# At six seams of a two-block kernel: scaled tiles in four buffers, scales issued ahead of the splits, transposes placed between the row-by-row products

## The reference, cut to what matters

```python
def first_block(x, c, ...):
    for l in range(2):
        sh_m, sc_m, gt_m, sh_f, sc_f, gt_f = split(silu(c) @ ada_w[l] + ada_b[l], 6)
        h = rmsnorm(x, norm_mix[l]) * (1 + sc_m) + sh_m          # seam ("mix", l)
        x = x + gt_m * hybrid_mixer(h, w_in[l], w_out[l], ...)   # attention, HGRN2, gated delta
        h = rmsnorm(x, norm_ffn[l]) * (1 + sc_f) + sh_f          # seam ("ffn", l)
        x = x + gt_f * ((silu(h @ w_gate[l]) * (h @ w_up[l])) @ w_down[l])

def second_block(x, mem, ...):
    for l in range(2):
        proj = x @ w_in_2[l]                                     # seam ("proj", l)
        out = merge(ssd(proj), diff_attention(proj), memory_attention(proj, mem)) @ w_out_2[l]
        x = layernorm(ALPHA * x + out, ln_g_2[l], ln_b_2[l])
```

## Time and profile before

| | |
|---|---|
| median of three runs | 4295.01 us |
| the three runs | 4287.96, 4295.93, 4295.01 us |
| span of the profiled execution (first to last instruction) | 4287.7 us |
| PE busy | 3992.2 us, 93% |
| DVE busy | 2571.8 us, 60% |
| ACT busy | 1621.0 us, 38% |
| mean granted clock of TensorE, share of full speed | 0.955 |

### The profile page before, as it was taken

One profiled execution on the slowest core, in us unless ns is written; L12 is line 12 of the kernel. 1 busy time (PEld: TensorE's weight loads), 2 busy tenths in 40 slices (PEclk: granted clock), 3 DMA queues, 4 the chain that ended last, 5 costly groups with the idle time before them and its releaser, 6 DMA issues.

```text
span 4287.7 us, 51835 instructions
## 1 busy us (share of the span) xinstructions
PE 3992.2 (93%) x20700; PEld 3250.2 (76%) x20700; DVE 2571.8 (60%) x4066; ACT 1621.0 (38%) x2881; POOL 108.0 (3%) x199
## 2 busy tenths in 40 slices
PE   5879999998889999999999999999899999999988
PEld 5759778877768788887777677767777777777776
DVE  6767365654576432456667743776566667546765
ACT  3343232243443332333444243553334343334532
POOL 0000000000000000000000000000000000000000
PEclk9979799998899799989999999999899999999999
DMA  6502155532111232333232223233232322221233
GB/s 219 171 5 89 50 168 196 188 118 65 60 40 69 72 101 84 106 100 104 91 99 72 74 89 94 64 104 126 80 119 85 108 70 84 84 88 56 84 113 113
DMA packets 216641, 417.93 MB, mean 97 GB/s; under 512 B 16384, under 2 KB 61472, under 8 KB 214608
## 3 DMA queue, kind: packets, MB, share of 16 engines
q1 hardware_dynamic: 197584, 335.12, 24.4%
q0 software_dynamic: 18816, 79.49, 5.4%
HBM read 378.89 MB, written 35.67 MB: 97 GB/s over the span
## 4 chain that ended last, share of the span: by engine, by line
PE 80%; DVE 12%; ACT 5%; issue 2%; DMA 1%; SPq 0%; DVEq 0%; ACTq 0%; POOLq 0%
PE ps L632 59%; PE ps L104 13%; DVE arena L126 3%; PE ps L115 3%; ACT arena L200 3%; DVE arena L141 2%; DVE spl L126 2%; PE ps L2292 2%; DVE X L126 1%; DVE HF L126 1%; DVE sm L147 1%; PE ps L2287 1%; ACT sph L200 1%; PE ps L882 1%; PE ps L110 1%
## 5 line engine op out<-in xcount | busy, mean ns | idle before, releaser
L126 DVE TENSOR_TENSOR spl<-ring,sph 128x1024 fp32r<-128x1024 f32 (+2 forms) x556 | 651.5, 1178 | 731.9 <-ACT sph L200 730.7
L200 ACT ACTIVATE sph<-ring 128x1024 fp32r<-128x1024 f32 (+2 forms) x556 | 562.4, 1023 | 776.6 <-PE ps L632 758.3
L632 PE MATMUL ps<-sph,HTh 128*128 128x512 f32 (+3 forms) x1680 | 668.9, 398 | 22.6 <-DVE HTl L126 11.7
L632 PE MATMUL ps<-spl,HTh 128*128 128x512 f32 (+3 forms) x1680 | 621.5, 370 | 0.0
L632 PE MATMUL ps<-sph,HTl 128*128 128x512 f32 (+3 forms) x1680 | 620.6, 369 | 0.0
L200 ACT ACTIVATE arena<-ps 128x512 f32<-128x512 f32 (+2 forms) x570 | 314.0, 563 | 727.8 <-PE ps L632 484.3
L632 PE MATMUL ps<-HTh,sph 128*128 128x512 f32 x1360 | 540.5, 397 | 17.1 <-DVE spl L126 14.9
L632 PE MATMUL ps<-HTl,sph 128*128 128x512 f32 x1360 | 532.5, 392 | 0.0
L632 PE MATMUL ps<-HTh,spl 128*128 128x512 f32 x1360 | 532.1, 391 | 0.0
L104 PE MATMUL ps<-arena 128*128 128x128 f32 (+6 forms) x2264 | 374.0, 349 | 52.3 <-ACT arena L200 29.9
L632 PE MATMUL ps<-sph 128*128 128x512 f32 x992 | 405.6, 409 | 7.4 <-DVE spl L126 7.4
(11 more groups left out here) (219 smaller groups left out, 5105.3 us busy)
## 6 DMA issues: line engine op xcount, KB each, us to landing
ring<-in_w_in SPq DMA_DIRECT2D x264, 512.0 KB, 3.6
arena<-in_ada_w SPq DMA_DIRECT2D x88, 512.0 KB, 4.7
ring<-in_w_down SPq DMA_DIRECT2D x44, 512.0 KB, 3.3
ring<-in_w_gate SPq DMA_DIRECT2D x40, 512.0 KB, 3.8
ring<-in_w_up SPq DMA_DIRECT2D x40, 512.0 KB, 3.8
ring<-in_w_mem SPq DMA_DIRECT2D x32, 512.0 KB, 3.3
ring<-in_w_out SPq DMA_DIRECT2D x32, 512.0 KB, 3.9
ring<-in_w_br_ssd SPq DMA_DIRECT2D x32, 512.0 KB, 3.9
```

The lines of the kernel that those rows point to most:

```text
L126: self.e.tensor_tensor(o, a, b, op).then_inc(*self.done.up())
L200: self.e.activation(o, a, f, **kw).then_inc(*self.done.up())
L632: ins = pe.e.matmul(o, l, r, start=k0 == 0 and i == 0 and not b.pairs, stop=k0 + b.ks == b.kt and i == 3 * b.ks - 1 and (c0 > 0 or not b.p ...
```

## The change

The scale's scratch grows from two buffers to four, in all three places where it is declared or used. On ACT the scale of tile k is issued ahead of the high half of tile k - 1, and on DVE the scale of tile k ahead of the rest of tile k - 2. The scales no longer wait for the engine's own last instruction. The rest of the second weight chunk moves from ahead of tile 2's scale to behind tile 2's rest, and that of the third from ahead of tile 4's scale to ahead of the rest of tile 7. On PE one turning stands ahead of each row k of the first products.

```diff
@@ first_products
             for k in range(b.ks):
+                next(turned[key], None)
                 pe.wait_ge(at[key, "hth", k], at[key, "htl", k])
...
             ins.then_inc(*pe.done.up())
-            for _ in range(b.ks):
-                next(turned[key], None)

         def ht_act(a, key, scale, bias, scr, marks=None):
-            for k in range(8):
-                if k == 4:
+            for k in range(9):
+                if k == 5:
                     warm_up(a, key, 2, 3)
-                f = scr[:, k % 2, :]
-                if scale is None:
-                    a.wait_ge(at[key, "htt", k])
-                    f = bank_of[key, "ht", k][:, :]
-                elif k % 2:
+                if scale is not None and k % 2:
                     bank = bank_of[key, "ht", k]
-                    a.wait_ge(at[key, "htt", k], at[key, "htl", k - 2] if k > 1 else None)
+                    a.wait_ge(at[key, "htt", k], at[key, "htl", k - 4] if k > 3 else None)
                     a.wait_ge(*[at[x] for x in marks(k)])
-                    t = a.act(f, bank[:, :], ACT.Identity, scale=scale[:, k:k + 1], bias=bias[:, k:k + 1], par=k > 1)
-                    at["free", (key, "ht", k)] = t
-                    a.wait_ge(t)
-                else:
-                    a.wait_ge(at[key, "htf", k])
-                at[key, "hth", k] = a.cp(HT[0][:, k, :], f, par=True)
+                    at[key, "htf", k] = at["free", (key, "ht", k)] = a.act(
+                        scr[:, k % 4, :], bank[:, :], ACT.Identity, scale=scale[:, k:k + 1], bias=bias[:, k:k + 1], par=True)
+                if k > 0:
+                    f = scr[:, (k - 1) % 4, :]
+                    if scale is None:
+                        a.wait_ge(at[key, "htt", k - 1])
+                        f = bank_of[key, "ht", k - 1][:, :]
+                    else:
+                        a.wait_ge(at[key, "htf", k - 1])
+                    at[key, "hth", k - 1] = a.cp(HT[0][:, k - 1, :], f, par=True)

         def ht_dve(v, key, scale, bias, scr):
-            for k in range(8):
-                if k in (0, 2, 4):
-                    warm_up(v, key, k // 2, k // 2 + 1)
-                f = scr[:, k % 2, :]
-                if scale is None:
-                    f = bank_of[key, "ht", k][:, :]
-                elif k % 2 == 0:
+            for k in range(10):
+                if k in (0, 5, 9):
+                    warm_up(v, key, k // 4, k // 4 + 1)
+                if scale is not None and k < 8 and k % 2 == 0:
                     bank = bank_of[key, "ht", k]
-                    v.wait_ge(at[key, "htt", k], at[key, "htl", k - 2] if k > 1 else None)
-                    t = v.ts(f, bank[:, :], scale[:, k:k + 1], bias[:, k:k + 1], ALU.mult, ALU.add, par=k > 1)
-                    at[key, "htf", k] = at["free", (key, "ht", k)] = t
-                v.wait_ge(at[key, "hth", k])
-                at[key, "htl", k] = v.tt(HT[1][:, k, :], f, HT[0][:, k, :].bitcast(F32), ALU.subtract, par=True)
+                    v.wait_ge(at[key, "htt", k], at[key, "htl", k - 4] if k > 3 else None)
+                    at[key, "htf", k] = at["free", (key, "ht", k)] = v.ts(
+                        scr[:, k % 4, :], bank[:, :], scale[:, k:k + 1], bias[:, k:k + 1], ALU.mult, ALU.add, par=True)
+                if k > 1:
+                    f = bank_of[key, "ht", k - 2][:, :] if scale is None else scr[:, (k - 2) % 4, :]
+                    v.wait_ge(at[key, "hth", k - 2], at[key, "htf", k - 2] if scale is not None else None)
+                    at[key, "htl", k - 2] = v.tt(HT[1][:, k - 2, :], f, HT[0][:, k - 2, :].bitcast(F32), ALU.subtract, par=True)
...
-            scr = ar(4096, 2, 512)
+            scr = ar(4096, 4, 512)
...
-            scr = ar(0, 2, 512)
+            scr = ar(0, 4, 512)
```

More of the change, by code:

```diff
@@ L905, in ht_act @@
-                at[key, "hth", k] = a.cp(HT[0][:, k, :], f, par=True)
-        def ht_dve(v, key, scale, bias, scr):
-            for k in range(8):
-                if k in (0, 2, 4):
-                    warm_up(v, key, k // 2, k // 2 + 1)
-                f = scr[:, k % 2, :]
-                if scale is None:
-                    f = bank_of[key, "ht", k][:, :]
-                elif k % 2 == 0:
-                    bank = bank_of[key, "ht", k]
-                    v.wait_ge(at[key, "htt", k], at[key, "htl", k - 2] if k > 1 else None)
-                    t = v.ts(f, bank[:, :], scale[:, k:k + 1], bias[:, k:k + 1], ALU.mult, ALU.add, par=k > 1)
-                    at[key, "htf", k] = at["free", (key, "ht", k)] = t
-                v.wait_ge(at[key, "hth", k])
-                at[key, "htl", k] = v.tt(HT[1][:, k, :], f, HT[0][:, k, :].bitcast(F32), ALU.subtract, par=True)
-                if scale is None:
-                    at["free", (key, "ht", k)] = at[key, "htl", k]
+                    at[key, "htf", k] = at["free", (key, "ht", k)] = a.act(
+                        scr[:, k % 4, :], bank[:, :], ACT.Identity, scale=scale[:, k:k + 1], bias=bias[:, k:k + 1], par=True)
@@ new lines, in ht_act @@
+                if k > 0:
[6 more added lines that the diff above has]
+                    at[key, "hth", k - 1] = a.cp(HT[0][:, k - 1, :], f, par=True)
+        def ht_dve(v, key, scale, bias, scr):
+            for k in range(10):
+                if k in (0, 5, 9):
+                    warm_up(v, key, k // 4, k // 4 + 1)
+                if scale is not None and k < 8 and k % 2 == 0:
+                    bank = bank_of[key, "ht", k]
+                    v.wait_ge(at[key, "htt", k], at[key, "htl", k - 4] if k > 3 else None)
[5 more added lines that the diff above has]
+                    at[key, "htl", k - 2] = v.tt(HT[1][:, k - 2, :], f, HT[0][:, k - 2, :].bitcast(F32), ALU.subtract, par=True)
+                    if scale is None:
+                        at["free", (key, "ht", k - 2)] = at[key, "htl", k - 2]
```

## The result

The changed kernel takes 4266.48 us in the median of four runs (4258.74 to 4274.89), the kernel before 4295.03. The ratio is 0.9943, with a 95% interval of 0.9922 to 0.9963. So it is faster, by 28.6 us, where 13.4 were forecast, and outside the range on its fast side.

A forecast was written before the change was run, and what follows sets the result against it. PE was taken as the bound, with 80% of the chain that ended last. Orders of -11.3 us and a clock term of -2.1 gave -13.4, taken off the median 4295.0: 4282 us, range 4272 to 4292.

The forecast's parts named there:

- The orders in the mixer seams: Mixer seams: reordered instructions start the second chunk earlier, -5.7 us in ("mix", 0) and -3.4 us in ("mix", 1).
- price of 1.47 us: Seam ("mix", 0): twelve products of one k take 1.47 us on PE.
- The clock behind the two waits: Behind both mixer-seam waits of 5.84 us: less low clock, bounds 0 and -4.2 us, taken at -2.1.
- the term -2.6: Seam ("proj", 1): rest 7 ends earlier, 3076.8 against 3079.45, and PE's start moves by the whole, -2.6 us.
- 3073.9: Seam ("proj", 1): time of the last turning's end, from 3073.4 plus some 0.5 us waiting for rest 0.
- the term 0: Seam ("proj", 0): tile 4's turning needs rest 0, which the first product needs anyway, so 0 us.
- the clock stays low: Rival, chance 0.11: strewn turnings delay the clock's rise at six seams, 1.6 us each, +9.6 against -11.3, about 4293.
- The ("ffn") seams: Both feed-forward seams: PE is the bound, the first product waits 0.2 us more, +0.2 us each.
- the thin cover: Seam ("ffn", 0): third chunk's weight rest done at about 589, PE wants it at 590.5, 1.5 us of cover.
- Between seams nothing: Stages between the six seams: no change expected, 0 us.
- slower rival: Rival, chance 0.04: a shift by 6 us makes more low clock in mixer stages, 130 to 325 us; say 4306.

The follow-up runs named there:

- PE's order alone: Kernel before with only the turnings of tiles 4 to 7 placed between the rows of the first products; 4277.48 us, ratio 0.9971.
- the buffers alone: Kernel before with four scale buffers and scales ahead of the splits, PE's order old; 4279.93 us, ratio 0.9978.
- the one with five added inside: Changed kernel plus five zero-adding products (1.1 us) at the start of layer 2's late mixer stage; 4272.8 us, ratio 0.9964.
- the row-wise kernel: Changed kernel with the second chunk's products multiplied row by row too in both mixer seams; 4276.24 us, ratio 0.9963.
- the one with ten added products: The row-wise kernel plus ten zero-adding products (2.2 us) at the start of layer 2's late mixer stage; 4264.18 us, ratio 0.9943.
- the fastest kernel: Changed kernel, second chunk row by row, tile 6's high half ahead of tile 7's scale, third weight rest ahead of rest 6; 4260.82 us, ratio 0.9935.
- the same with added work in layer 1: The fastest kernel plus twelve zero-adding products (2.6 us) behind seam ("mix", 0); 4275.01 us, ratio 0.9965.

## Why the prediction was right or wrong

**The orders in the mixer seams: right, in ("mix", 0) with luck.** From the first turning to the second chunk it is 57.53 - 43.20 = 14.33 us in ("mix", 0) and 966.07 - 949.49 = 16.58 in ("mix", 1). The kernel before took 19.99 and 20.30 there (its first turnings start at 43.80 and 958.94; the earlier trace rows have the ends). So -5.66 and -3.72, against -5.7 and -3.4. The wait left is 2.51 us, forecast 2.4. In ("mix", 1) the other three traces with the new seams agree (16.5 to 16.7 us). In ("mix", 0) only one does (14.2); the two others took 16.7 and 17.0. PE in the second profile of the changed kernel (changed again):

```profile
48.80 0.56 PE L883 MATMUL ps<-sph,HTh 128*128 128x256 f32 x1
49.16 0.41 PE L883 MATMUL ps<-sph,HTl 128*128 128x256 f32 x1
...
60.05 0.36 PE L632 MATMUL ps<-sph,HTh 128*128 128x256 f32 x1 [2.51 <-DVE HTl L126]
```

Here the first twelve products took 0.41 us each and started 0.21 apart, where in the first profile they took 0.28 and started 0.12 apart: the clock rose later in this execution. In the kernel before two of five traces have such slow first products too, and its seam took 20.0 us to the second chunk in all five, since the hand-over of tiles hid them. The change took that cover away. My price of 1.47 us for twelve products assumed the early rise, and -5.7 is about -3 without it.

**The clock behind the two waits: right in kind, mis-sized.** Behind them the seam gained a further 1.4 and 2.6 us in the first pair of profiles, and no trace with the new seams shows the low clock right behind either wait; the term was bounded at 0 to -4.2 and taken at -2.1, and nearly its outer bound came.

**("proj", 1): the term -2.6 was mis-sized; it was about -4.1.** Timeline of the changed kernel, PE and then DVE:

```profile
3036.42 4.12 PE L115 MATMUL ps<-cst,X 128*128 128x128 f32 x20 [6.61 <-ACT X L200]
3040.81 0.27 PE L883 MATMUL ps<-sph,HTh 128*128 128x64 f32 x1 [0.27 <-DVE HTl L126]
...
3043.90 1.09 PE L115 MATMUL ps<-cst,X 128*128 128x128 f32 x8
...
3052.80 0.42 PE L632 MATMUL ps<-sph,HTh 128*128 128x64 f32 x1 [2.48 <-DVE spl L126]
```

```profile
3047.32 0.68 DVE L126 TENSOR_TENSOR HTl<-arena,HTh 128x512 fp32r<-128x512 f32 x1
...
3052.47 0.28 DVE L126 TENSOR_TENSOR spl<-ring,sph 128x128 fp32r<-128x128 f32 x1
```

From the last turning (3044.99) to the end of rest 7 (3048.00) it is 3.0 us, as forecast (2.9). The failed step is "3073.9" for the end of that turning: I let the turnings keep the low-clock price of the earlier trace rows, 3.17 us for sixteen. But the clock had risen by then: eight take 1.09. DVE's list behind rest 7 is full as before and passes the whole of it on to PE, as the prediction said.

**("proj", 0): the term 0 was wrong, since the clock was left out of it.** PE before, then after:

```profile
1854.93 2.98 PE L115 MATMUL ps<-cst,X 128*128 128x128 f32 x16 [2.08 <-DVE X L126]
1857.56 0.40 PE L882 MATMUL ps<-sph,HTh 128*128 128x64 f32 x1
...
1862.68 3.51 PE L115 MATMUL ps<-cst,X 128*128 128x128 f32 x16
```

```profile
1831.00 3.86 PE L115 MATMUL ps<-cst,X 128*128 128x128 f32 x20 [2.08 <-DVE X L126]
...
1835.13 0.28 PE L883 MATMUL ps<-sph,HTh 128*128 128x64 f32 x1
...
1836.13 0.66 PE L115 MATMUL ps<-cst,X 128*128 128x128 f32 x4
...
1837.89 1.09 PE L115 MATMUL ps<-cst,X 128*128 128x128 f32 x8
```

Before, products and turnings run at the low clock (0.40 a product, 3.51 for sixteen turnings); in the changed kernel both are at full clock from the fourth product on. The orders there were hidden, as I wrote, but the clock rose earlier in the seam, which was worth 3.3 us, and PE's order alone gives as much (40.9). That the strewn turnings are the cause is not shown: with the buffers alone the turnings stand in blocks as before, and the seam took 39.8 in the one trace that there is. Once, in changed again, the clock stayed low through the whole seam, and it took 45.9, 1.7 more than before. That is the rival "the clock stays low", at its own price of 1.6 us, in one of four traces and at one seam. As a whole the rival fell: in the four traces with the new seams the low clock in the two ("proj", l) seams was less than before in seven of eight cases, with turnings strewn among the products. The rule behind it was that of the Trainium skill, "TensorE: Matmul & The Clock Gate", Part 4, by which turnings do not count as busy in the same way; where it and these seams differ, the measurement decides.

**The ("ffn") seams:** forecast +0.2 each, measured 0.0 and +0.5. No wait for a weight rest appeared; the thin cover held.

**"Between seams nothing": this is the step that failed most.** The late mixer stage of layer 2 gave 8.3 us. I had the mechanism in the text only as the slower rival ("a shift by 6 us could make more of it"), looked for it at 130 to 325 us, where the length stayed within 1.5 us, and gave it one sign. It works, at another place, and here it had the other sign. That a shift of the seam's end can cause it is borne out by the kernel before with 1.1 us added right behind the seam, which took the changed kernel's course in its trace and became faster in its twelve executions (4.7 us by the ratio, 0.4 to 9). The changed kernel's own traces all entered the stage in one way (last low stretch 33.8 or 33.9 us ahead of it, in three of three, the one with five added inside among them), those of the kernel before never (7.3 to 14.7 in four of four). That the new seam brings the short course rests on these seven. It is no rule for every execution: the row-wise kernel and the one with ten added products are the same program up to this stage, and entered it in the two different ways. Why the clock stays low for 41.0 us on one course and 23.9 on the other, with PE busy throughout, no run here tells.

**What stays open.** For layer 1's late stage the traces give 229 to 243 us with old seams and 229 to 236 with new ones; whether the 4 us between the means belong to the change is not settled. Why the clock rises early in one execution of ("mix", 0) or ("proj", 0) and late in another is not known either. And the seam's length is not the only thing that picks the course: with ("mix", 1) at 45.4 us in both, the fastest kernel took 218.8, the same with added work in layer 1 225.0.

**The sum.** By the table, forecast against measured: the two mixer seams with their clock -11.2 and -12.4, ("proj", 1) -2.6 and -4.1, ("proj", 0) 0 and -2.0, the ("ffn") seams +0.4 and +0.5, between the seams 0 and -8.3 in layer 2, with the open -4 of layer 1. So the seams alone would have ended inside the range; what carried the time out of it is the term "between seams nothing". The range had a slip of its own: it speaks of 3 us of run-to-run spread below, but its lower end is worked out with 8.

## What to carry to other kernels

Cost a seam instruction by instruction from its handing-over rows, and use the prices of the clock that will hold after the change, not of the one before. Where TensorE goes between its two clocks far from the change, a shift of one microsecond can be worth several of either sign: ask which stages run near such a change, and widen the range by it both ways. Before crediting or blaming an edit of this size, cut the traces at the same instructions, and see whether a bare delay does the same.

## What the runs showed of the hardware

The low clock held for 41.0 us in one piece while PE was busy for 40.71 of them, in a stage of narrow products and short chains (64 columns in most of them); it is not only idle time that keeps the clock low. The other way round, PE stood idle for 2.51 us after a stretch at full clock at both mixer seams of the changed kernel, and the clock stayed at 1.00 behind it in all four traces; idle times of 5.84 us at the same places cost it in the kernel before. Where the changes fall is not the same in two executions, but it is not free either: kernels with unlike programs ahead showed the same course, with low stretches at 118.5, 119.0 or 136.9 us and lengths equal to 0.1 us. The page "TensorE: Matmul & The Clock Gate" of the Trainium skill (Part 1) says that the monitor behind the clock runs on its own and does not start with the kernel, so that the place of a change differs from run to run. The traces agree, and add that here it is worth 214.8 to 228.0 us in one stage whose instructions are all the same.
